# Two-layer hybrid decoder trunk: the opening of the even layer ordered anew, its S5 tables and scan computed by the vector engine

## What is computed

```python
mod = silu(c) @ ada_w[i] + ada_b[i]          # six parts of 1024: shift, scale, gate (mixer), and the same (FFN)
hn = rms_norm(h, norm_mix_w) * (1 + sc_m) + sh_m
proj = hn @ w_in                             # q, k, v, z (512 each), beta and decay (4 + 4), u (512)
qkv = silu(causal_conv4(proj[q, k, v]))      # per channel, four taps
# S5: 32 groups of 16 channels, each with a complex diagonal state of 64
lb = exp(lam * dt);  bb = (lb - 1) / lam * b
x_t = lb * x_(t-1) + bb u_t;  y = Re(c x) + d u;  y_s5 = glu(gelu(y))
h = h + gt_m * (concat(gated_delta_net(q, k, v, z, beta, g), y_s5) @ w_out)
```

## Time and profile before

| | us |
|---|---|
| median of 3 runs | 1559.36 (1557.35 to 1566.99) |
| the profiled execution | 1569.96 |
| its span | 1568.4 |
| PE busy | 1415.3 (90%) |
| DVE busy | 771.9 (49%) |
| ACT busy | 503.9 (32%) |
| GpSimd busy | 215.3 (14%) |

### The profile page before, as it was taken

One profiled execution on the slowest core, in us unless ns is written; L12 is line 12 of the kernel. 1 busy time (PEld: TensorE's weight loads), 2 busy tenths in 40 slices (PEclk: granted clock), 3 DMA queues, 4 the chain that ended last, 5 costly groups with the idle time before them and its releaser, 6 DMA issues.

```text
span 1568.4 us, 17805 instructions
## 1 busy us (share of the span) xinstructions
PE 1415.3 (90%) x6956; PEld 1183.2 (75%) x6956; DVE 771.9 (49%) x762; ACT 503.9 (32%) x569; POOL 215.3 (14%) x256
## 2 busy tenths in 40 slices
PE   2479968968997899999999999999986999999997
PEld 1357857857996688888888878888775888888886
DVE  7792884065564646623366552444446323333243
ACT  3225320044413332212222234566524222222232
POOL 5891991034000000000000000000000000000000
PEclk6577985678999899989999979999997999999999
DMA  9117756310011447623374322211122232342321
GB/s 323 50 47 106 228 169 172 81 54 1 1 55 27 134 142 233 227 77 98 107 232 168 109 81 81 81 55 49 33 81 81 80 107 74 93 128 80 87 84 71
DMA packets 205705, 164.12 MB, mean 105 GB/s; under 512 B 29601, under 2 KB 195714, under 8 KB 203602
## 3 DMA queue, kind: packets, MB, share of 16 engines
q1 hardware_dynamic: 202416, 137.25, 30.7%
q0 software_dynamic: 2720, 25.99, 4.6%
q10 hardware_dynamic: 514, 0.12, 0.1%
HBM read 158.23 MB, written 4.19 MB: 104 GB/s over the span
## 4 chain that ended last, share of the span: by engine, by line
PE 78%; POOL 8%; DVE 6%; issue 4%; ACT 3%; DMA 1%; SPq 0%; DVEq 0%; ACTq 0%; POOLq 0%
PE banks L467 21%; PE banks L468 21%; PE banks L469 21%; PE banks L688 4%; DMA ada_first<-in_ada_w_dram 1%; DVE hn_lo L1547 1%; PE banks L659 1%; PE banks L661 1%; PE banks L922 1%; PE banks L949 1%; POOL scan_a L2107 1%; PE banks L663 1%; PE banks L542 1%; POOL scan_a L2108 1%; POOL scan_a L2102 1%
## 5 line engine op out<-in xcount | busy, mean ns | idle before, releaser
L467 PE MATMUL banks<-hn_hi,whi 128*128 128x512 f32 x992 | 393.0, 396 | 5.0 <-DVE hn_lo L1547 4.9
L468 PE MATMUL banks<-hn_lo,whi 128*128 128x512 f32 x992 | 390.6, 394 | 0.0
L469 PE MATMUL banks<-hn_hi,wlo 128*128 128x512 f32 x992 | 389.9, 393 | 0.0
L1515 DVE TENSOR_TENSOR wlo<-raw,whi 128x2048 fp32r<-128x2048 f32 (+3 forms) x107 | 232.0, 2169 | 145.0 <-ACT whi L1103 83.9
L467 PEld LDWEIGHTS banks<-hn_hi,whi 128*128 128x128 f32 x992 | 189.1, 191 | 48.4 <-issue 9.2
L1109 ACT ACTIVATE whi<-raw 128x2048 fp32r<-128x2048 f32 (+1 forms) x66 | 123.1, 1866 | 316.9 <-PE banks L469 315.8
L469 PEld LDWEIGHTS banks<-hn_hi,wlo 128*128 128x128 f32 x992 | 189.1, 191 | 40.2
L468 PEld LDWEIGHTS banks<-hn_lo,whi 128*128 128x128 f32 x992 | 189.3, 191 | 39.0
L467 PE MATMUL banks<-ff_hi,whi 128*128 128x512 f32 x416 | 163.9, 394 | 0.0
L469 PE MATMUL banks<-ff_hi,wlo 128*128 128x512 f32 x416 | 162.7, 391 | 0.0
L468 PE MATMUL banks<-ff_lo,whi 128*128 128x512 f32 x416 | 162.6, 391 | 0.0
(11 more groups left out here) (409 smaller groups left out, 1923.3 us busy)
## 6 DMA issues: line engine op xcount, KB each, us to landing
raw<-in_ffn_w_in_dram SPq DMA_DIRECT2D x88, 512.0 KB, 4.9
ada_in<-in_ada_w_dram POOLq DMA_DIRECT2D x16, 1536.0 KB, 6.4
ada_in<-in_ada_w_dram SPq DMA_DIRECT2D x32, 512.0 KB, 4.1
raw<-in_ffn_w_out_dram SPq DMA_DIRECT2D x32, 384.0 KB, 3.9
raw<-in_sb_w_in_dram SPq DMA_DIRECT2D x24, 512.0 KB, 4.4
raw<-in_hy_w_in_dram SPq DMA_DIRECT2D x20, 512.0 KB, 5.9
raw<-in_ffn_w_out_dram SPq DMA_DIRECT2D x32, 320.0 KB, 3.6
ada_first<-in_ada_w_dram SPq DMA_DIRECT2D x4, 2048.0 KB, 18.6
```

The source lines that it names most:

```text
L467: pe.matmul(o, lh, rh, start=first, stop=False)
L468: pe.matmul(o, lh, rl, start=False, stop=False)
L469: return pe.matmul(o, ll, rh, start=False, stop=last)
L1515: TTO(wlo[s][:, 0:width], raw[s][:, 0:width], whi[s][:, 0:width].bitcast(F32), SUB)\
```

## The change

- Norm of the first layer: x is squared and scaled as tokens (`x_sq`, `x_tok`) by ACT and transposed a second time to `x_n`; the path over `sq_sum`, `diag` and a broadcast product goes. `hn_hi` is one activation from `x_n`, `hn_lo` two DVE operations; U blocks 0 and 1 take the tiles as they come.
- S5 parameters are transposed first by PE (three transposes of `lam_raw`) and all powers and factors made on 128x16 by DVE. GpSimd's powers, V tables and scan are gone. DVE makes V in four parts (`v_rows`), W in four (`w_rows`) between convolutions of block 1.
- The scan over chunks becomes a turn by a table (`turn_cos`, `turn_sin`, built by doubling), 32 real scans of 64 elements (`tensor_tensor_scan`) and a turn back, all on DVE (`states_turned`), between the convolutions of blocks 8 to 11.
- The taps, W transposes and S5 chunk inputs come behind q/k/v blocks 0 to 7 instead of before block 0. Taps and transposes use three banks in turn instead of two. ACT's gate functions move behind the second set of convolutions.
- `ada_first` is eight transfers of 1 MB into four tiles of their own, without a wait. The tiles of parts 2 to 4 are loaded behind `scan_done`, those of part 5 behind the loads of y. The modulation columns of parts 2 and 3 stand between the third and the fourth bank of the y products, those of 4 and 5 behind the z blocks.
- The loads of c move from GpSimd's queue to ACT's.

The core of the diff (SP, PE, ACT, DVE in this order):

```diff
+            for g in range(8):
+                rows = ada_w[0].rearrange("(p t) n -> p t n", t=8)[:, 2 * (g % 4):2 * (g % 4) + 2, :]
+                sp.dma_start(ada_first[g // 2][:, 2 * (g % 2):2 * (g % 2) + 2, :],
+                             rows[:, :, (g // 4) * D:(g // 4 + 1) * D]).then_inc(first_ld[g], 16)
                 if g == 3:
...
+            for n in range(4, 6):
+                load_slot(n, n % 2, cols(w, 256 * (n - 2))(n % 2))
...
-            sp.wait_ge(w_done, 8)
+            sp.wait_ge(v_done, 1)
...
+            for n in range(6, 8):
+                load_slot(n, n % 2, cols(w, 256 * (n - 2))(n % 2))
...
-            for n in range(4, 8):
-                load_slot(n, n % 2, cols(w, 256 * (n - 2))(n % 2))
-                for i in range(2 if n < 6 else 4):
-                    if n < 6:
-                        ada0_tile(2, 4 + 2 * (n - 4) + i)
-                    else:
-                        ada0_tile(3, 4 * (n - 6) + i)
             load_slot(8, 0, cols(w, 256 * 6)(0))
             load_slot(9, 1, cols(w, 256 * 7)(1))
-            for part in range(4, 6):
+            sp.wait_ge(scan_done, 1)
+            for part in range(2, 5):
                 for t in range(8):
                     ada0_tile(part, t)
...
+            for t in range(8):
+                ada0_tile(5, t)
...
+            pe.wait_ge(dt_done, 1)
+            for n in range(3):
+                last = pe.transpose(bank[5][:, 16 * n:16 * n + 16], lam_raw[:, n, :], ident[0:16, 0:16])
+            last.then_inc(lam_t, 1)
...
+            for k in range(KT):
+                pe.wait_ge(xn_tok, TT)
+                pe.wait_ge(x_done, min(KT, k + 5))
+                if k >= 4:
+                    pe.wait_ge(xn_done, k - 3)
...
+            pe.wait_ge(xn_done, KT)
+            as_tiles_come(0, B_U, 0, (0, 1), lambda w_: w_[:, :].rearrange("p (k two m) -> p k two m", k=KT, two=2))
...
+            four_blocks(2, B_QKV, hn_hi, hn_lo)
+            four_blocks(4, B_QKV + 4, hn_hi, hn_lo)
...
+                b = 4 + q % 3
+                if q >= 3:
+                    pe.wait_ge(k_done, q - 2)
...
+            four_blocks(6, B_QKV + 8, hn_hi, hn_lo)
...
+                if q == 3:
+                    mod_parts(2, ada0_acc, (24, 32))
+                    pe.wait_ge(mod_done, 2)
...
+            z_blocks(0)
+            z_blocks(1)
+            pe.wait_ge(y_done, 4)
+            mod_parts(4, ada0_acc, (40, 48))
...
+            for t in range(TT):
+                last = squares(t)
+            last.then_inc(ss_done, 1)
...
+            act.wait_ge(diag_done, 1)
+            for t in range(TT):
+                act.activation(x_tok[:, t, :], x_tok[:, t, :], ACT.Copy, scale=rstd[:, t:t + 1]).then_inc(xn_tok, 1)
+            for k in range(KT):
+                act.wait_ge(xn_t, k + 1)
+                act.activation(x_n[:, k, :], bank[k % 4], ACT.Copy).then_inc(xn_done, 1)
...
+            for k in range(KT):
+                act.activation(hn_hi[:, k, :], x_n[:, k, :], ACT.Identity, bias=mod[:, k:k + 1],
+                               scale=n_scale[:, k:k + 1]).then_inc(hi_norm, 1)
...
+            act.preload_act_table(ACT.Silu)
+            qkv(0)
+            qkv(1)
+            act.wait_ge(g_abs, 1)
+            step(act.activation(g_t[0][:, :, :], g_t[0][:, :, :], ACT.Exp, scale=-1.0))
+            act.activation(g_t[0][:, :, :], g_t[0][:, :, :], ACT.Ln, bias=ONE_C).then_inc(g_ln, 1)
+            act.activation(beta[:, :, :], ba[:, :, 0:NH], ACT.Sigmoid).then_inc(beta_done, 1)
...
+                TS(tmp[k % 2][:, :], x_n[:, k, :], n_scale[:, k:k + 1], mod[:, k:k + 1], MUL, ADD)\
+                    .then_inc(h_scaled, 1)
+                dve.wait_ge(hi_norm, k + 1)
+                dve.wait_ge(h_scaled, k + 1)
+                TTO(hn_lo[:, k, :], tmp[k % 2][:, :], hn_hi[:, k, :].bitcast(F32), SUB).then_inc(hn_done, 1)
...
+            def v_rows(which, half):
+                ii = slice(8 * half, 8 * half + 8)
+                def c4(x_):
+                    return x_[:, ii, :].unsqueeze(2).to_broadcast([P, 8, SC + 1, GH])
+                def p4(x_):
+                    return x_[:, :, ii].rearrange("p k i -> p i k").unsqueeze(3).to_broadcast([P, 8, SC + 1, GH])
+                dst, a_, b_ = ((v_re, c_re, nc_im), (v_im, nc_im, nc_re))[which]
+                t_, d_ = v_t[:, :, :, :], dst[:, ii, :, :]
+                dve.wait_ge(c_done, 1)
+                step(TTO(t_, c4(b_), p4(pw_im), MUL))
+                step(TTO(d_, c4(a_), p4(pw_re), MUL))
+                last = TTO(d_, d_, t_, ADD)
...
+            def turn_tables():
+                step(TTO(decay[:, :], lam[:, 6, :], lam[:, 6, :], MUL))
+                step(TTO(decay[:, :], decay[:, :], decay[:, :], MUL))
+                step(TTO(decay[:, :], decay[:, :], decay[:, :], MUL))
+                doubled(lam[:, 10:12, :])
+                doubled(turn_n)
+                doubled(turn_n)
+                dve.memset(turn_cos[:, :, 0], 1.0)
+                step(dve.memset(turn_sin[:, :, 0], 0.0))
+                n = 1
+                while n < NC:
+                    shape = [P, PAIRS, n]
+                    c_, s_ = (turn_n[:, q, :].unsqueeze(2).to_broadcast(shape) for q in range(2))
+                    c0, s0 = turn_cos[:, :, 0:n], turn_sin[:, :, 0:n]
+                    c1, s1 = turn_cos[:, :, n:2 * n], turn_sin[:, :, n:2 * n]
+                    w_ = turn_t[:, :, 0:n]
+                    step(TTO(w_, s0, s_, MUL))
+                    step(TTO(c1, c0, c_, MUL))
+                    step(TTO(c1, c1, w_, SUB))
+                    step(TTO(w_, c0, s_, MUL))
+                    step(TTO(s1, s0, c_, MUL))
+                    step(TTO(s1, s1, w_, ADD))
+                    n *= 2
+                    if n < NC:
+                        doubled(turn_n)
...
+            v_rows(0, 0)
+            v_rows(0, 1)
+            lo(2, 0)
+            lo(3, 1)
+            v_rows(1, 0)
+            v_rows(1, 1)
...
+                def scans(dst, src, lo_):
+                    for i in range(lo_, lo_ + 8):
+                        last = dve.tensor_tensor_scan(dst[:, i, :], decay[:, i:i + 1].to_broadcast([P, NC]),
+                                                      src[:, i, :], 0.0, MUL, ADD)
+                    step(last)
+                if at_ == 0:
+                    dve.wait_ge(p_done, 4)
+                    step(TTO(a, re, c_, MUL))
+                elif at_ == 1:
+                    step(TTO(b, im, s_, MUL))
+                    step(TTO(a, a, b, ADD))
+                elif at_ == 2:
+                    step(TTO(b, re, s_, MUL))
+                    step(TTO(re, im, c_, MUL))
+                elif at_ == 3:
+                    step(TTO(im, re, b, SUB))
+                    scans(s_re, scan_a, 0)
...
+                elif at_ == 10:
+                    TTO(re, b, a, SUB).then_inc(scan_done, 1)
...
+            for r in range(4):
+                conv_block(0, r)
+            w_rows(0, 0)
+            w_rows(0, 1)
+            conv_block(1, 0)
+            w_rows(1, 0)
+            conv_block(1, 1)
+            conv_block(1, 2)
+            conv_block(1, 3)
+            w_rows(1, 1)
...
+            turn_tables()
+            states_turned(0)
+            states_turned(1)
+            states_turned(2)
+            conv_block(2, 0)
+            for at_ in (3, 4, 5):
+                states_turned(at_)
+            conv_block(2, 1)
+            for at_ in (6, 7, 8):
+                states_turned(at_)
+            conv_block(2, 2)
+            for at_ in (9, 10):
+                states_turned(at_)
+            conv_block(2, 3)
+            for part in range(2, 4):
+                for t in range(8):
+                    ada0_tile(part, t)
```

More of the change, by code:

```diff
@@ L584, in _ @@
             last.then_inc(ba_rows, 1)
-            four_blocks(0, B_U, hn_hi, hn_lo, first=True)
+            slot_ready(1)
+            for j in range(2):
+                gemm(2 + j, 1, j, hn_hi, hn_lo)
             pe.wait_ge(ba_copied, 1)
@@ L1075, in _, with c_parts @@
             act.activation(c_act[:, :], c_col[:, :], ACT.Silu).then_inc(c_ready, 1)
+            def c_parts():
+                act.wait_ge(c_t, 1)
+                for par in range(2):
+                    rows = slice(64 * par, 64 * par + 64)
+                    for dst, b, scale in ((c_re, 4, 1.0), (nc_re, 4, -1.0), (nc_im, 5, -1.0)):
+                        src = bank[b].rearrange("p (i two h) -> p i two h", two=2, h=GH)[rows, :, par, :]
+                        last = act.activation(dst[rows, :, :], src, ACT.Copy, scale=scale)
+                last.then_inc(c_done, 1)
@@ L1089, in _ @@
-            for par in range(2):
-                rows = slice(64 * par, 64 * par + 64)
-                for dst, b, scale in ((c_re, 4, 1.0), (nc_re, 4, -1.0), (nc_im, 5, -1.0)):
-                    src = bank[b].rearrange("p (i two h) -> p i two h", two=2, h=GH)[rows, :, par, :]
```

(7 more changed lines are left out.)

510 lines of the change are left out of this document (215 added, 295 removed).

## The result

The changed kernel takes 1576.31 us (median of three runs, 1575.72 to 1578.68) against 1559.36: ratio 1.0091, 95% interval 1.0052 to 1.0131. It is slower by 0.9%, where 1554.0 was predicted with a range of 1537 to 1572. The profiled execution took 1578.68 us, span 1577.1; that of the kernel before 1569.96 and 1568.4. So the two profiles differ by 8.7 us and the medians by 17.0; both numbers need an explanation. Some 3 us of the 17.0 are in the three runs of the kernel before: 31 of its runs, taken beside the experiments, have a median of 1562.6.

What follows compares the result with a forecast made beforehand. GpSimd's work in the opening was taken as the bound, then the ada tiles behind the states. First reduce 6.8 us earlier, less 1.5 for half-clock turns, nets -5.3: 1554 us from the median 1559.36; range 1537 to 1572.

Steps and rivals of the forecast that it cites:

- What bounds: Opening up to the first GDN reduce: GpSimd's work makes PE wait 21.2 us for `s_im` and 16.2 us for `hn_lo`.
- S: Time at which `scan_done` comes, the chunk states being ready: predicted 207.8 us, against 241.2 before.
- What becomes late next: Behind `scan_done`: all 32 ada tiles of parts 2 to 5 at 2.72 us each; most of the gain goes there.
- To the modulation: Kernel start to modulation: DVE's row ends last near 45.9, PE's columns take 3.57; modulation at 49.7 us instead of 52.3.
- U to the states: U blocks, q/k/v blocks, taps, S5 inputs, turn tables and scans: U ends at 81.4, states ready at 207.8 us.
- Behind the states: Ada tiles, y transfers and last modulation columns: first reduce at S+111.8, 319.6 us against 326.42.
- third rival: Ada tiles land slower, over 2.9 us each instead of 2.72: 1560 to 1579 us; chance 0.20.
- fourth rival: States stay near 241 us because something uncosted in DVE's queue takes 30 us: 1590 us; chance 0.03.
- The 1.5 us for half-clock turns: Start of GDN: PE's twelve turns at the lower clock take 1.12 us instead of 0.66; 1.5 us charged.
- The step to the median: Whole kernel: the 5.3 us gain, from an execution 10.6 above the median, taken off the median 1559.36: 1554 us.
- The rival in which the gain is kept: Behind the states PE's y and z, not the ada chain, bound: reduce at 299 us, time 1532; chance 0.08.

Runs made afterwards that it cites:

- The repaired kernel: Changed kernel with c_raw and y transfers on GpSimd's queue, four tile buffers, and two z blocks ahead of the states: 1532.7 us, ratio 0.9804 to the kernel before.

## Why the prediction was wrong, point by point

*What bounds.* Right: GpSimd's table work went, S moved forward, and the last modulation columns behind the row of tiles became the bound ("What becomes late next"). The tables' move to DVE cost what it was priced at.

*To the modulation: the first step that failed.* "Modulation at 49.7"; measured 61.2. The step counted DVE's row and ACT's norm, but not the four c_raw issues that ScalarE had been given, nor TensorE's turns of c_raw between x tiles 3 and 4. Of the 11.5 us, 2.2 are DVE's own row (51.9 with everything else removed), 8.0 are DVE's later start, behind the sines that ScalarE's issues hold (26.1 instead of 18.05), and 1.3 are DVE's wait for the root of the norm, behind the landing of c_raw. The two are chains of nearly one length: issuing later alone gave nothing (64.9), the landing alone was worth 1.2 (53.1 to 51.9), both together 9.3. DVE's own 2.2 lie in the 37 angle steps, which end at 17.1 and not at 15.7 even where nothing holds them (six take 0.30 to 0.64 us), and at 18.0 where the sines wait for them. The profile of before had the price of a c_raw issue only on GpSimd's queue, 0.77 us each; the edit that moved the loads was priced at nothing.

*U to the states.* Right in length: 158.1 us predicted from modulation to S, 156.5 measured. U blocks end at 93.2 (81.4 and the 11.5 make 92.9), the taps' copies start at 149.1 (139) and are 2.54 apart (2.55), the S5 inputs are down at 175.0 (169 + 11.5 less 5.5, since the W copies were quicker), DVE idled 14.2 (13) for the gate sums, the turn tables took 22.5 (23.2). A scan takes 0.198 us (0.2 taken, 0.14 to 0.5 as bounds). The Trainium skill, "DVE: opcode table, instruction layouts, handler registers and perf-mode slots", section "Datapath and trigger behaviour", says that the built-in scan runs at half throughput; the prediction's estimate from it, about 0.2 us, agrees with the trace. The formula of the Trainium skill, "VectorE: DVE Perf Modes", section "The TRN2 errata — SBUF-src ops pay a fixed extra latency per instruction", gives an estimated 174 ns for 16 elements, and the busy time is 0.17 us. The tables cost the 0.21 us from one step to the next, as the prediction had it. S: 217.7 for 207.8.

*Behind the states.* Right in kind, short by 5.6 us: first reduce at S+117.4, predicted S+111.8. Tiles 16 to 31 S+46.0 (45.3), fourth bank S+63.3 (62.4), tile 39 S+69.6 (67), y loads issued S+82.5 (79.7), tile 47 S+108.7 (102.9). The pace of a tile was right: 2.72 was taken, and start to start it is 2.67, 2.64 and 2.78 in the three parts of the row. So the third rival (tiles slower than 2.9) did not occur, though the time fell into its range; that is chance. What failed is the row around the tiles. About 2.1 us are late by tile 39's issue, since DVE first waits 3.7 us for the columns of parts 2 and 3 (267.44 above), which the prediction let run beside the tiles. The y transfers took 0.7 more. The last eight tiles took 26.2 us from the end of the y loads' issue where 23.2 were taken: 1.4 because the first of them came on DVE 5.5 us behind its issue and not 4.1, 0.4 in pace, and 1.3 because the sum left out the time of the last tile itself. The fourth rival (S stays at 241) did not occur. The 1.5 us for half-clock turns did not come: from the first reduce to the root's table load it is 8.2 us after and 8.6 before, and to the end 1242.0 in both.

So between the profiled executions: 9.9 (S) + 5.6 (the row) - 1.5 (turns) = 14.0, and -5.3 + 14.0 = +8.7, which is what the two traces show.

*The step to the median.* The other 8.2 of the error of 22.3. The sum was made against an execution 10.6 us above its median and the difference was carried over unchanged. But that execution was long in the very stretch that the change rebuilds: TensorE was the bound there in the kernel before, at a granted clock of 0.72, and another execution, at 0.94, has its first reduce at 317.3, not 326.4. The changed kernel has 0.73 and 0.77 in the same stretch in its two profiles and TensorE busy for 22.5 of 30 us, waiting for others, and its execution lay 2.4 above its median. TensorE is not the bound there, so the change had nothing to win back in that stretch against a shorter execution; this is argued from the traces and not tried. Against the shorter execution even the predicted 319.6 would have been 2.3 us late, not 6.8 early: "the same 5.3 off the median" booked as a gain what only the long execution had to give. Some 3 of the 8.2 us are the median of three runs (1559.4, where 31 runs have 1562.6).

*The rival in which the gain is kept* (1532, "If the ada chain were not the bound") was refused for this kernel rightly, by the order of the queue. The repaired kernel ends at 1532.7, but by other changes on top (buffers, queues, z blocks), so that the two numbers meet is chance.

## What to carry to other kernels

A DMA moved to the queue of another engine can take that engine's time, here 13.6 us: price its issue there, then look up who reads its data, and what stands behind that reader in program order. A chain that names one wait can hide another close beside it: here the chain went through c_raw's landing, taking the landing out of it alone was worth 1.2 us, and the rest came only with the engine's hold gone too. Four loads of 128 KB cost 8 to 9 us of a 1560 us kernel in either version. When work is gathered behind one event, count the queue behind it: two buffers and foreign transfers in the row made 117 us of what took 77 with four buffers, the transfers on an idle queue and two blocks moved into the wait. And take more than one execution of the baseline when its runs spread: a gain is worth only what the typical execution spends in that stretch.

## What was unexpected of the hardware

- Four loads of 128 KB took 8.2 us for the last issue, with 4.5 more for the next load behind, on ScalarE's queue, and landed 14.6 to 22.4 us after issue; on GpSimd's queue the same four took 0.77 to 0.80 us each and landed in 8.4 to 9.8. The Trainium skill, "DMA: Bandwidth & Descriptors", section "Issuing engine by pattern", says that the queues of SyncE and ScalarE are generally the faster and GpSimd's the more flexible, and its section "Issuing engines are not separate DMA queues" that the time to initiate a DMA is usually small beside the DMA itself: for these loads the measurement goes against both, and decides. The hold went with these loads when their place changed (9.41 for the c_im pair behind the vectors, 9.32 in the kernel before), and the one load directly behind them, which had taken 0.32, took over 4. ScalarE's queue carried 0.64 MB in 2626 packets in all, and 0.12 MB in 514 without them. Whether their short rows or their place in the traffic make the hold was not tried.
- TensorE's lower clock level came while it was fully busy. With z blocks directly ahead of the y products, stretches of that run show:
```profile
209.50:215.00 5.50, 5.50 (x33) 4.64 (x32) 5.36 (x6) 0.63 (x1) 0.00 (x0) 1.00 0.82 290
215.00:222.00 7.00, 7.00 (x34) 6.04 (x33) 5.95 (x5) 0.60 (x1) 0.00 (x0) 0.65 0.92 316
222.00:247.00 25.00, 25.00 (x92) 21.50 (x91) 12.69 (x11) 0.60 (x1) 0.00 (x0) 0.50 0.74 268
```
  the y products begin, at 211.7, at the upper level (1.00) and fall to the lower (0.50) with no idle time between. In the other traces that were read by stretch, y ran at the lower level from the start.
- With four tiles of 512 KB in flight instead of two, the median landing rose only from 4.3 to 5.0 us (longest 5.5 and 7.8), and the stretch from 217 to 282 moved 241 GB/s instead of 196 (186 in the first profile of the changed kernel).
